# A two-layer hybrid decoder trunk on one core: the fourth gate unit of each attention issued in pieces inside it

## The reference

```python
g_a, g_b, g_c, g_d = _split(jax.nn.sigmoid(p_gate.astype(F32)).astype(x.dtype), GATE_SPLITS)
merged = g_a * y_a + g_b * y_b + g_c * y_c + g_d * y_d
x = x + merged @ w_o[l]
...
sc = jnp.where(key_pos[None, :] <= q_pos[:, None], sc, NEG_INF)
pr = jax.nn.softmax(sc, axis=-1)
return jnp.einsum('bhqk,bkhd->bqhd', pr.astype(v.dtype), v)
```

## Time and profile before

| what | value |
|---|---|
| median of 3 runs | 2073.06 us (2071.59 to 2074.18) |
| time of the profiled execution | 2073.46 us |
| its span, first to last instruction | 2071.6 us |
| mean granted TensorE clock | 0.991 |
| PE busy | 1995.8 us, 96% of the span |
| weight loads (PEld) busy | 1535.3 us, 74% |
| DVE, ACT, POOL busy | 52%, 36%, 36% |

### The profile page before, as it was taken

How to read it: one execution, slowest core, us unless ns; L and a number is a source line. 1 busy time by engine, 2 the same in 40 slices (tenths; PEclk the granted TensorE clock), 3 DMA queues, 4 the chain that set the end, 5 groups by cost and what they waited for, 6 DMA issues and landing times.

```text
span 2071.6 us, 31700 instructions
## 1 busy us (share of the span) xinstructions
PE 1995.8 (96%) x13128; PEld 1535.3 (74%) x13128; DVE 1077.2 (52%) x1794; ACT 757.2 (37%) x1180; POOL 737.8 (36%) x550
## 2 busy tenths in 40 slices
PE   5999999999999999999989899999999999999997
PEld 4778787756667888888867777776566778888886
DVE  6685654896833422222367766369976343222223
ACT  4542513344353432322253353134344433322322
POOL 2540313322324444444435122143213344444442
PEclk8999999999999999999999999999999999999998
DMA  5320112221312333233332111123122222323231
GB/s 192 104 79 27 55 47 61 82 80 49 120 49 77 115 94 100 93 101 95 98 112 85 51 37 57 39 80 100 51 71 86 66 91 93 100 93 101 92 99 64
DMA packets 52254, 170.20 MB, mean 82 GB/s; under 512 B 5648, under 2 KB 13968, under 8 KB 51472
## 3 DMA queue, kind: packets, MB, share of 16 engines
q1 hardware_dynamic: 50928, 163.11, 24.6%
q0 software_dynamic: 1184, 5.07, 0.6%
HBM read 160.82 MB, written 7.34 MB: 81 GB/s over the span
## 4 chain that ended last, share of the span: by engine, by line
PE 87%; DVE 8%; ACT 3%; issue 1%; DMA 1%; SPq 0%; DVEq 0%; ACTq 0%
PE bank_a L476 14%; PE bank_a L477 13%; PE bank_a L482 13%; PE bank_v L482 7%; PE bank_v L476 7%; PE bank_v L477 7%; PE bank_v L542 4%; PE bank_v L620 3%; PE bank_a L762 1%; PE bank_f L574 1%; PE bank_f L580 1%; PE bank_f L553 1%; PE bank_a L751 1%; DVE arena L1444 1%; PE bank_f L575 1%
## 5 line engine op out<-in xcount | busy, mean ns | idle before, releaser
L437 POOL TENSOR_TENSOR w_lo<-ring,w_hi 128x512 fp32r<-128x512 f32 x536 | 731.4, 1385 | 1236.6 <-ACT w_hi L1132 1236.6
L476 PE MATMUL bank_a<-h_hi,w_hi 128*128 128x512 f32 x1312 | 530.8, 405 | 6.6 <-ACT w_hi L1132 6.6
L477 PE MATMUL bank_a<-h_lo,w_hi 128*128 128x512 f32 x1312 | 512.7, 391 | 0.0
L1132 ACT ACTIVATE w_hi<-ring 128x1024 fp32r<-128x1024 f32 x268 | 281.5, 1050 | 215.3 <-DVE arena L2012 212.4
L482 PE MATMUL bank_a<-h_hi,w_lo 128*128 128x512 f32 x1312 | 324.6, 389 | 0.0
L476 PEld LDWEIGHTS bank_a<-h_hi,w_hi 128*128 128x128 f32 x1312 | 247.2, 188 | 77.8 <-issue 19.4
L477 PEld LDWEIGHTS bank_a<-h_lo,w_hi 128*128 128x128 f32 x1312 | 247.3, 188 | 58.2 <-issue 8.1
L482 PEld LDWEIGHTS bank_a<-h_hi,w_lo 128*128 128x128 f32 x1312 | 246.0, 188 | 50.9
L476 PE MATMUL bank_v<-parts,w_hi 128*128 128x512 f32 x640 | 250.7, 392 | 1.4 <-DVE parts L1983 1.4
L477 PE MATMUL bank_v<-parts,w_hi 128*128 128x512 f32 x640 | 249.0, 389 | 0.0
L1444 DVE TENSOR_TENSOR sg<-bank_v,sg 128x512 f32<-128x512 f32 x112 | 77.5, 692 | 317.3 <-PE bank_v L482 245.8
(11 more groups left out here) (286 smaller groups left out, 2449.7 us busy)
## 6 DMA issues: line engine op xcount, KB each, us to landing
ring<-in_w SPq DMA_DIRECT2D x268, 512.0 KB, 3.5
out_ring<-in_w SPq DMA_DIRECT2D x64, 128.0 KB, 3.4
x_dram<-arena SPq DMA_DIRECT2D x2, 2048.0 KB, 9.6
arena<-x_dram SPq DMA_DIRECT2D x2, 2048.0 KB, 9.0
arena<-in_x SPq DMA_DIRECT2D x2, 1024.0 KB, 8.9
arena<-tabs POOLq DMA_DIRECT2D x4, 512.0 KB, 4.8
out_x<-arena SPq DMA_DIRECT2D x2, 1024.0 KB, 4.6
par<-in_par POOLq DMA_DIRECT2D x2, 937.0 KB, 7.4
```

The lines of the kernel that those rows point to most:

```text
L437: ins = nc.gpsimd.tensor_tensor(w_lo[:, g % SPLIT, ks, :], raw, w_hi[:, g % SPLIT, ks, :].bitcast(F32), ALU.subtract)
L476: mm(b[:], w_hi[:, s, k, :], hi[:, k, :], start=k == 0, stop=False)
L477: mm(b[:], w_hi[:, s, k, :], lo[:, k, :], start=False, stop=False)
L1132: act_fn(w_hi[:, g % SPLIT, :, :], ring[:, g % RING, :, :], ACT.Copy).then_inc(S["split_hi"], 1)
```

## The change

The fourth unit of each attention is also run in pieces, so each attention has four units, 24 pieces. Steps 1 to 12 still take one piece each; steps 13 to 18 take two. The whole unit behind the attention is gone on PE, and ACT copies the fourth unit raw and takes four sigmoids afterwards in place of three and one. `mg_raw` counts 8 copies in a layer in place of 6. The number of matmuls, loads and transfers is the same.

```diff
-GATE_STEPS = tuple(range(1, 19))
+GATE_STEPS = tuple(range(1, 13)) + tuple(i for i in range(13, 19) for _ in range(2))
+GATE_ENDS = GATE_STEPS[5::6]
...
             def gate_pieces(l, br, i, numbers):
 
-                for j in range(3):
+                for j in range(4):
                     g = begin_unit(("merge", br, i + j), l)
...
                 attention(l, "m", lambda h, qt: Mv["q"][0:96, h, qt * P:(qt + 1) * P],
-                          lambda h, n: Mv["k"][0:96, h, 0:n], lambda i: next(pieces) if i in GATE_STEPS else None)
-                numbers.append(gate(l, 1, 3))
+                          lambda h, n: Mv["k"][0:96, h, 0:n], lambda i: [next(pieces) for _ in range(GATE_STEPS.count(i))])
                 pe.wait_ge(S["m_y"], at(l, "m_y", 8))
...
-                if i in GATE_STEPS and GATE_STEPS.index(i) % 6 == 5:
+                if i in GATE_ENDS:
                     act.wait_ge(f_full, filled_f.next())
-                    n = sigs[0] + GATE_STEPS.index(i) // 6
+                    n = sigs[0] + GATE_ENDS.index(i)
...
                 attention(l, "m", Mv, 0, lambda i: piecewise_sig(l, i))
-                late_sig(l, 3)
-                merge_sig(l, 1)
+                late_sig(l, 4)
                 merge_sig(l)
```

More of the change, by code:

```diff
@@ L280, in build @@
             ("m_ss", 16), ("m_p", 16), ("m_n", 16), ("m_pt", 16), ("m_y", 8),
-            ("mg_sig", 32), ("mg_raw", 6), ("mg_done", 32), ("mg_hi", 8), ("mg_lo", 8), ("wo_done", 8), ("up_relu", 32), ("up_sq", 32), ("up_hi", 32), ("up_done", 32), ("g_zs", 1), ("r_s0", 1), ("g_s0", 1), ("down_done", 8 * QUARTERS),
+            ("mg_sig", 32), ("mg_raw", 8), ("mg_done", 32), ("mg_hi", 8), ("mg_lo", 8), ("wo_done", 8), ("up_relu", 32), ("up_sq", 32), ("up_hi", 32), ("up_done", 32), ("g_zs", 1), ("r_s0", 1), ("g_s0", 1), ("down_done", 8 * QUARTERS),
         ):
@@ L1001, in _ @@
                 attention(l, "d", lambda h, qt: Dv["q"][quarter(h % 2), h // 2, qt * P:(qt + 1) * P],
-                          lambda h, n: Dv["k"][quarter(h % 2), h // 2, 0:n], lambda i: next(pieces) if i in GATE_STEPS else None)
-                numbers.append(gate(l, 3, 3))
+                          lambda h, n: Dv["k"][quarter(h % 2), h // 2, 0:n], lambda i: [next(pieces) for _ in range(GATE_STEPS.count(i))])
                 pe.wait_ge(S["d_y"], at(l, "d_y", 8))
@@ L1118, in late_sig @@
                 act.wait_ge(S["mg_raw"], at(l, "mg_raw", n))
-                for _ in range(3):
+                for _ in range(4):
                     n = sigs[0]
@@ L1381, in _ @@
                 attention(l, "d", Dv, 1, lambda i: piecewise_sig(l, i))
-                late_sig(l, 6)
-                merge_sig(l, 1)
+                late_sig(l, 8)
                 mg_tile = 0
```

## The result

| | before | after |
|---|---|---|
| median, 10 runs each | 2072.66 us | 2078.1 us |
| profiled execution | 2073.46 us | 2077.22 us |
| its span | 2071.6 us | 2075.4 us |
| four attention places in the trace (below), sum | 203.88 us | 208.15 us |

The ratio of the times is 1.0026, with a 95% interval of 1.0016 to 1.0036: the change made the kernel 0.26% slower. One run of the changed kernel was disturbed and is left out of the ratio. The forecast was 2077.8.

The account below looks back on a forecast made before the run. PE, busy for 96% of the span, was taken to bound the kernel. Each attention: -5.35 + 5.45 + 0.58 + 0.51 = +1.19 us; four, +4.8, take 2073.06 to 2077.8 us (8 in 10: 2073.8 to 2080.6).

Parts of the forecast that it names:

- PE is full in the last steps: In attention m's last steps PE is busy 12.42 of 12.9 us; one 0.5 us wait, nothing left for a second piece.
- `bank_f` wait: Unit 3's first matmul in step 16 waits for ACT to copy unit 2's bank: 0.58 us, between 0 and 1.17.
- `yo` wait: The outputs behind the last results wait for ACT's last copy into `yo`: 0.51 us, between 0 and 0.86.
- six pieces in place of the unit: In each attention, six more pieces add 5.45 us and the whole unit behind it removes 5.35: +0.10 us.
- The wait rows that the prediction named as signs: In each attention, new PE waits of about 0.6 us in step 16 (`bank_f`, 8 to 12) and 0.5 for `yo`.
- rival of the hidden gaps: Second pieces fill gaps in the last steps, winning back 1.9 us for each attention: 2070 us, not slower; chance 0.12.
- rival of the missing wait: One of the two new waits doesn't show; an attention costs 0.6 to 0.7 us: 2075.6 us, same; chance 0.10.
- rival of a late DVE: Behind m, DVE uses up its 2.02 us in hand and 1.5 more in each layer: 2080.9 us, slower; chance 0.10.
- DVE's time in hand at the last merge of m: Of 2.02 us at the last merge, DVE has 0.9 us less for its selection, but PE is later by 1.2.
- the 0.9 us by which DVE's end in the attention was to move: The extra piece in step 13 delays the scores of pairs 14 and 15, and so DVE's end, by 0.9 us.
- ACT's split in step 15: ACT's split of unit 4 (1.06 us) comes in step 15 in place of step 18 and costs nothing.
- the fourth sigmoid: Behind each attention it costs PE nothing; behind d DVE's first merge can start some 4 us after the last results.

Follow-up runs that it names:

- e5: The changed kernel, leaving out 12 of the 24 matmuls of unit 3 in attention d of both layers; 2073.0 us.
- e1: The changed kernel with the last of the 24 pieces issued on PE behind the last results and ahead of the outputs; 2075.9 us.
- e2: The changed kernel with the same 24 pieces in other steps, so that units end in steps 5, 9, 13 and 18; 2070.1 us.
- e7: The changed kernel with units ending in steps 5, 9 and 13, two pieces in step 5, and the last piece behind the last results; 2072.7 us.
- e3: The changed kernel with the second pieces in steps 1 to 6 and not in 13 to 18; 2076.1 us.
- e4: The changed kernel with units ending in steps 5, 9 and 13, two pieces in step 1, and the last piece behind the last results; 2068.0 us.
- e6: The kernel before, three units in pieces and the fourth whole behind the attention, with units ending in steps 5, 11 and 18; 2067.1 us.
- e10: e7 with five of DVE's selection steps taken from behind attention m into it; 2067.8 us.

## Why the prediction was right

**PE is full in the last steps: shown for d.** e5 took 12 matmuls out of each of two places and got 12 times the distance between two matmuls back.

**The terms.** In m, layer 0, the place grew by 1.06 us; the forecast was 1.19. The `bank_f` wait was forecast at 0.58 and measured at 0.59; the `yo` wait 0.51 and 0.46. What is left for six pieces in place of the unit is 1.06 - 0.59 - 0.46 = 0.01 against 0.10. Both kinds of wait were then removed by themselves (e1, e2) and gave back 0.42 us for `yo` and 7.8/12 = 0.65 us for each wait at the bank. The wait rows that the prediction named as signs are shorter than its terms: the four new ones for `bank_f` make 5.6 - 4.3 = 1.3 us, 0.3 each, and those for `yo` 0.4 each. Its comparison of 0.58 with the 0.54 of the old rows set a price by loads beside one by rows. Four places make 4.27 us of the forecast 4.8; the profiled executions are 3.8 us apart and the medians 5.4, and what lies between is outside the places: it is not explained by them and is within what two executions differ by. So the size of the effect is right to about half a us, and that the forecast lies within 0.3 us of the median is in part luck: the places grew by 0.5 us less than forecast, and the rest of the program made up for it.

**The rival of the hidden gaps: refuted, by e5.** The Trainium skill (Perfetto Trace Analysis, "Identifying the Most-Contended Engine") takes the share of weight loads, beside the share of peak arithmetic, as the measure of TensorE's headroom. Here 69% beside 84% pointed to 1.9 us of room in each attention; e5 shows none. In the kernel before, the loads for the scores in those steps take 0.19 us and stand 0.43 us apart (511.53 and 511.96), where those of a gate unit stand 0.23 apart, and PE waits for nothing between them: the share is low there without idle time that a piece could use.

**The rival of the missing wait: refuted,** both are in the rows. **The rival of a late DVE: not in this kernel, but close.** The prediction said that DVE's time in hand at the last merge of m would grow, since PE would be later by more than DVE. It shrank from 2.02 to 1.31 us:

```profile
562.44 0.69 DVE L1441 TENSOR_TENSOR sg<-bank_v,sg 128x512 f32<-128x512 f32 x1 [1.31 <-PE bank_v L543]
```

This step of the working was wrong, without harm here. PE was later by 1.06 us, near the 1.2 of the prediction; the term that failed is the 0.9 us by which DVE's end in the attention was to move. DVE's last normalization waits for ACT's exponential of pair 15, and that stands behind ACT's copy of the results that PE makes behind the pieces of step 14. So the second piece of step 14 delays it as well as that of step 13. Before:

```profile
515.19 0.28 ACT L1169 ACTIVATE yo<-bank_a 128x128 f32<-128x128 f32 x1 [1.00 <-PE bank_a L762]
515.36 0.72 ACT L1157 ACTIVATE arena<-arena,att 128x512 f32<-128x512 f32 x1
...
516.20 0.16 DVE L1617 RECIPROCAL att<-att 128x1 f32<-128x1 f32 x1 [1.23 <-ACT arena L1157]
```

and after:

```profile
516.31 0.28 ACT L1168 ACTIVATE yo<-bank_a 128x128 f32<-128x128 f32 x1 [1.93 <-PE bank_a L763]
516.48 0.71 ACT L1156 ACTIVATE arena<-arena,att 128x512 f32<-128x512 f32 x1
...
517.32 0.16 DVE L1614 RECIPROCAL att<-att 128x1 f32<-128x1 f32 x1 [2.47 <-ACT arena L1156]
```

Counted from the first load of scores (482.28 and 481.56), that normalization begins at 33.92 us before and at 35.76 after, 1.84 later. 2.02 + 1.06 - 1.84 = 1.24 us, near the 1.31 that are left.

In the experiments with four units inside, this decided. More pieces stand ahead of DVE's last work in m: the same normalization begins at 37.0 us in e2 and e7, 38.5 in e3 and 36.1 in e4, and DVE reaches the last merges without any time in hand in all four. In e6, with three units inside, it begins at 33.3 us, and DVE has 2.00 us in hand, though PE saved 1.5 us in m just as in e7. So it wasn't PE's saving by itself that used up the time, but the pieces put ahead of DVE's work together with it. e10, e7 with less DVE work behind m, has 1.59 us in hand again, and the loss at the start of d is gone.

**What had been costed at nothing.** ACT's split in step 15 and the fourth sigmoid cost nothing that can be seen, as said: PE has no wait for either. DVE's first merge behind d started 3.75 us behind ACT's last copy into `yo` (611.66 to 607.91), near the "some 4 us" of the forecast, and nobody waited for it:

```profile
611.66 0.69 DVE L1441 TENSOR_TENSOR sg<-bank_v,sg 128x512 f32<-128x512 f32 x1 [13.64 <-ACT sg L1120]
```

## What to carry to other kernels

Work moved into a pipelined stretch gains only what an engine waits there; read the wait rows of that very stretch first, and count what the moved work was covering where it stood. With one accumulation bank for consecutive units, put the unit's end where other matmuls follow that are longer than the hand-over (here 1.17 us): that alone gave 6 to 8 us (e6, e2), where the place of the unit gave nothing. And look at how much time the next engine has in hand, both when you make the full engine quicker and when you put work ahead of what the next engine waits for. Beyond it the gain turns into idle time, and in e3, e4 and e7 the clock fell behind such idle time too.

## What was unexpected of the hardware

In e7, layer 0, PE had two waits of 1.72 and 0.81 us with a few small matmuls between them; the granted clock was at half (1.2 GHz) within the second, 0.50 from 566 to 567 us, and stayed there to 572. In layer 1 the same kernel had waits of 1.72 and 0.89 us, and the clock fell only at about 1583 us, some 1 us behind the second. In e4 two waits of 0.8 and 0.89 us were followed by half the clock in layer 1 but not in layer 0, and in e3 waits of 0.81 and 0.89 us in layer 0 but not in layer 1, though PE's rows before them look the same each time. So whether a short idle time costs the clock isn't decided by its length alone. No run here tells what decides it.
